# Second feed-forward stage on h times its weight, with the norm's scale at the gate

## The reference

```python
h = h + 0.5 * rmsnorm(swiglu(rmsnorm(h, gn[0]), ffn_w_in[0], ffn_w_out[0]), gn[1])   # first stage, 272 tokens
h = h + rmsnorm(mlstm_mixer(rmsnorm(h, gn[2]), ...), gn[3])                          # mixer
h = h + 0.5 * rmsnorm(swiglu(rmsnorm(h, gn[4]), ffn_w_in[1], ffn_w_out[1]), gn[5])   # second stage, 256 tokens
for l in range(2):                                                                   # two conditioned layers
    shift, scale, gate = split(silu(c) @ w_ada[l] + b_ada[l], 3)
    y = rms_norm(h, pre_norm_g[l]) * (1.0 + scale) + shift
    mix = attention_and_convolution(y @ w_in[l]) @ w_out[l]
    h = h + gate * rms_norm(mix, post_norm_g[l])

def rmsnorm(x, g):    # per token: x * rsqrt(mean(x * x) + 1e-6) * g
def swiglu(x, w_in, w_out):
    gu = x @ w_in
    return (silu(gu[..., :2816]) * gu[..., 2816:]) @ w_out
```

## Time and profile before

| | us |
|---|---|
| median of 3 runs | 833.57 (833.28 to 833.63) |
| profiled execution, whole time | 833.62 |
| its span (first to last instruction) | 831.7 |
| PE matmul busy / PE weight load busy | 803.1 / 777.6 |
| DVE busy | 584.6 |
| ACT busy | 418.5 |
| POOL busy | 128.0 |
| mean granted TensorE clock | 0.995 |
| DMA read and written | 158.96 MB |

### The profile page before, as it was taken

One profiled execution on the slowest core, in us unless ns is written; L12 is line 12 of the kernel. 1 busy time (PEld: TensorE's weight loads), 2 busy tenths in 40 slices (PEclk: granted clock), 3 DMA queues, 4 the chain that ended last, 5 costly groups with the idle time before them and its releaser, 6 DMA issues.

```text
span 831.7 us, 15721 instructions
## 1 busy us (share of the span) xinstructions
PE 803.1 (97%) x6436; PEld 777.6 (93%) x6436; DVE 584.6 (70%) x946; ACT 418.5 (50%) x716; POOL 128.0 (15%) x138
## 2 busy tenths in 40 slices
PE   7999999999999999999999999999999999999996
PEld 7999999999899899999999999989888999898895
DVE  6777776798687875788777768775666468566543
ACT  7544444445257665555444454445654365464541
POOL 3000000032210000010000012220235202025413
PEclk9999999999999999999999999999999999999998
DMA  9876676776245632459888775517444451734421
GB/s 326 295 254 221 226 249 242 226 274 201 88 143 185 196 112 93 152 186 340 291 287 270 275 238 185 184 51 256 150 124 150 154 173 55 259 130 147 131 76 51
DMA packets 45751, 158.96 MB, mean 191 GB/s; under 512 B 5064, under 2 KB 7624, under 8 KB 45680
## 3 DMA queue, kind: packets, MB, share of 16 engines
q1 hardware_dynamic: 45680, 157.96, 56.7%
HBM read 156.88 MB, written 1.06 MB: 190 GB/s over the span
## 4 chain that ended last, share of the span: by engine, by line
PE 76%; DVE 14%; ACT 6%; issue 2%; DMA 1%; POOL 1%; SPq 0%; DVEq 0%; ACTq 0%; POOLq 0%
PE ps L112 69%; PE ps L114 7%; DVE w L114 3%; ACT w L114 2%; DVE u L114 2%; DVE tmp L114 2%; DVE yg L114 1%; DVE Sb L114 1%; DVE st L114 1%; DVE cv L114 1%; ACT SW L114 1%; ACT Sb L114 1%; ACT L114 1%; DMA raw<-wst 1%; POOL rst L114 1%
## 5 line engine op out<-in xcount | busy, mean ns | idle before, releaser
L112 PE MATMUL ps<-u,w 128*128 128x256 f32 (+1 forms) x3887 | 499.9, 285 | 3.1 <-DVE w L114 1.6
L112 PEld LDWEIGHTS ps<-u,w 128*128 128x128 f32 x3887 | 481.9, 188 | 11.3 <-DVE w L114 4.0
L114 DVE TENSOR_TENSOR w<-raw,w 128x1024 fp32r<-128x1024 f32 x245 | 297.4, 1225 | 168.0 <-ACT w L114 161.6
L114 ACT CAST w<-raw 128x1024 fp32r<-128x1024 f32 x245 | 254.8, 1050 | 135.5 <-PE ps L114 124.8
L112 PE MATMUL ps<-h,w 128*128 128x272 f32 (+1 forms) x1000 | 130.4, 285 | 0.0
L112 PEld LDWEIGHTS ps<-h,w 128*128 128x128 f32 x1000 | 126.1, 188 | 0.1
L114 POOL TENSOR_TENSOR sqa<-sqa,sq 128x256 f32<-128x256 f32 (+1 forms) x22 | 23.1, 1050 | 358.3 <-ACT sq L114 357.8
L114 POOL TENSOR_SCALAR Sb<-Sb,st 128x256 f32<-128x256 f32 x32 | 42.9, 1355 | 111.1 <-DVE st L114 111.1
L114 DVE SCALAR_TENSOR_TENSOR acc<-adr,cact,acc 128x1024 f32<-128x1024 f32 x42 | 56.4, 1353 | 0.3 <-DMA adr<-wada 0.3
L114 PE MATMUL ps<-u,w 128*128 128x256 f32 (+1 forms) x169 | 48.1, 284 | 0.0
L112 PE MATMUL ps<-m,w 128*128 128x256 f32 x368 | 46.7, 281 | 0.0
(11 more groups left out here) (175 smaller groups left out, 692.2 us busy)
## 6 DMA issues: line engine op xcount, KB each, us to landing
raw<-wst SPq DMA_DIRECT2D x245, 512.0 KB, 4.6
adr<-wada SPq DMA_DIRECT2D x48, 512.0 KB, 4.0
Bt<-bias_rows SPq DMA_DIRECT2D x8, 192.0 KB
hT<-xT SPq DMA_DIRECT2D x4, 272.0 KB, 4.9
outT<-hT SPq DMA_DIRECT2D x2, 384.0 KB, 2.6
outT<-hT SPq DMA_DIRECT2D x1, 256.0 KB, 2.6
cs<-cst SPq DMA_DIRECT2D x1, 140.0 KB, 6.3
cs<-cst SPq DMA_DIRECT2D x1, 128.0 KB, 7.2
```

The costliest lines, as they stand in the source:

```text
L112: fn()
L114: fn().then_inc(m[0], m[1])
```

## The change

The second stage now works as the first does. u1 and u2 are made of the new h times the weight, without the second scale. The second scale is still made, and used in two places: as the factor r0 at each gate, and, since the up half and so the stage's output stay unscaled, through eps in the next norm: eps0 = (mean square + eps) * eps, which the first conditioned layer's boundary adds in place of eps.

- rms_pair is cut in two. rms_first makes the first scale; rms_second the mean square and the second power, without its transposes.
- add_and_weigh takes the place of add_and_normalise at this boundary. For each k: yg times the scale and the addition as before; then ACT writes u1 = h * gain, and DVE writes u2 = h * gain - u1. rms_second and the eps0 product stand behind the second addition in the queues.
- Its spread_scale goes to head as a hook: ahead of the head's fifth k PE transposes the second scale into bank 5, and DVE copies it into r0.
- In ffn both stages multiply the gate by r0 on DVE (zg), and silu reads zg.
- The second stage's modulation steps follow the first's pattern: 14 in the gates' loop (before 21), and 3, 3, 2 and 2 behind the first four output rows (before 1, 1, 1 and 0).

```diff
@@ rms_pair
-        def rms_pair(n, eps_of=None):
+        def rms_first(n, eps_of):
...
             dense(4)
-            r1 = spread(6, n, rst, m1)
+            state["bc"] = r1 = spread(6, n, rst, m1)
+            return r1, m1, mc
+
+        def rms_second(n, m1, mc):
...
             m2 = state["pow2"] = pool(partial(nc.gpsimd.tensor_tensor, rst2[:, 0:nt], msh[:, 0:nt], eps3[:, 0:nt],
                                               ALU.pow), mt, state.get("bc2"))
+            return m2, mt
+
+        def rms_pair(n, eps_of=None):
+
+            r1, m1, mc = rms_first(n, eps_of)
+            m2, _ = rms_second(n, m1, mc)
             dense(6)
-            r2 = spread(5, n, rst2, m2)
-            state["bc"], state["bc2"] = r1, r2
+            r2 = state["bc2"] = spread(5, n, rst2, m2)
             return r1, r2
@@ new, behind add_and_normalise
+        def add_and_weigh(n, off, ygm, hm, gain):
+
+            r1, m1, mc = rms_first(n, None)
+            mul, res, scale = {}, {}, {}
+
+            def scaled(k):
+                mul[k] = dve(partial(nc.vector.tensor_tensor, yg[:, k, 0:n], yg[:, k, 0:n], ps[:, 6, 0:n], ALU.mult),
+                             r1, ygm[k])
+                eng, e = (dve, nc.vector) if k in (0, 4) else (pool, nc.gpsimd)
+                res[k] = eng(partial(e.tensor_tensor, hT[:, k, off:off + n], hT[:, k, off:off + n], yg[:, k, 0:n],
+                                     ALU.add), mul[k], hm[k])
+
+            scaled(0)
+            for k in range(KT):
+                if k < KT - 1:
+                    scaled(k + 1)
+                if k == 0:
+                    scale["pow"], m = rms_second(n, m1, mc)
+                    dve(partial(nc.vector.tensor_scalar, eps0[:, 0:2], msh[:, 0:2], EPS, None, ALU.mult), m)
+                h, u = hT[:, k, off:off + n], u1[:, k, 0:n]
+                um1[k] = act(partial(nc.scalar.mul, u, h, gain(k)), res[k], ustate["use"])
+                um[k] = dve(partial(nc.vector.scalar_tensor_tensor, u2[:, k, 0:n], h, gain(k), u.bitcast(F32),
+                                    ALU.mult, ALU.subtract), um1[k])
+            free[6] = mul[KT - 1]
+
+            def spread_scale(i):
+                if i == KT // 2:
+                    m = state["bc2"] = spread(5, n, rst2, scale["pow"])
+                    first["r"] = free[5] = dve(partial(nc.vector.tensor_copy, r0[:, 0:n], ps[:, 5, 0:n]), m)
+
+            return [res[k] for k in range(KT)], spread_scale
@@ ffn
-                head(x1, x2, n, um1, um, nb=4)
+                head(x1, x2, n, um1, um, hook=hook, nb=4)
...
-                if j and (n == S or j % 3):
+                if j % 3:
                     ada_step(acc)
...
-                if n == S:
-                    s = free[bg] = act(partial(nc.scalar.activation, si[:, i, :], ps[:, bg, 0:n], ACT.Silu), mg,
-                                       hfr[i])
...
-                    z = free[bg] = dve(partial(nc.vector.tensor_tensor, zg[:, i, :], ps[:, bg, 0:n], r0, ALU.mult),
-                                       mg, first["r"], sir[i])
-                    s = sir[i] = act(partial(nc.scalar.activation, si[:, i, :], zg[:, i, :], ACT.Silu), z, hfr[i])
+                z = free[bg] = dve(partial(nc.vector.tensor_tensor, zg[:, i, 0:n], ps[:, bg, 0:n], r0[:, 0:n],
+                                           ALU.mult), mg, first["r"], sir[i])
+                s = sir[i] = act(partial(nc.scalar.activation, si[:, i, :], zg[:, i, 0:n], ACT.Silu), z, hfr[i])
...
-                while j < 4 and 0 < ad["use"] % 24 < ((17, 20, 22, 24) if n == T else (22, 23, 24, 24))[j]:
+                while j < 4 and 0 < ad["use"] % 24 < (17, 20, 22, 24)[j]:
@@ calls
-        hm = add_and_normalise(S, 16, ygm, hm, vg(4), None)
+        hm, hook = add_and_weigh(S, 16, ygm, hm, vg(4))
...
-        ygm = ffn(S, lambda j: gh[:, 8 + j:9 + j], guard, hm, 16, w_ffn[1])
+        ygm = ffn(S, lambda j: gh[:, 8 + j:9 + j], guard, hm, 16, w_ffn[1], hook)
...
-                                   lambda k: mod[:, 24 * l + k:24 * l + k + 1], m_G[l])
+                                   lambda k: mod[:, 24 * l + k:24 * l + k + 1], m_G[l], None if l else eps0)
```

More of the change, by code:

```diff
@@ L515, in rms_pair @@
                         state["sum"], state.get("pow"))
-                m = dve(partial(nc.vector.tensor_tensor, sst[0:16, 2:3], ps[0:16, 7, 4:5], eps_of[0:16, 2:3],
-                                ALU.add))
+                if nt == 3:
+                    m = dve(partial(nc.vector.tensor_tensor, sst[0:16, 2:3], ps[0:16, 7, 4:5], eps_of[0:16, 2:3],
+                                    ALU.add))
             m1 = state["pow"] = pool(partial(nc.gpsimd.tensor_tensor, rst[:, 0:nt], sst[:, 0:nt], eps3[:, 0:nt],
@@ L528, in rms_pair @@
             dense(4)
-            r1 = spread(6, n, rst, m1)
+            state["bc"] = r1 = spread(6, n, rst, m1)
+            return r1, m1, mc
+        def rms_second(n, m1, mc):
+            nt = len(sum_tiles(n))
             rows = [P, P, 16]
@@ L745, in build, with ffn @@
         br_m = {}
-        def ffn(n, gh_of, guard, hm, off, gw):
+        def ffn(n, gh_of, guard, hm, off, gw, hook=None):
             fx = ExitStack()
```

## The result

The changed kernel takes 835.32 us (median of 11, 834.09 to 837.12), the kernel before 833.36 (11, 832.94 to 834.19): ratio 1.0024, 95% interval 1.0015 to 1.0032. It is slower by 1.96 us, just above the 0.2% that count as a change. It is inside the stated range (832.8 to 835.8), 1.2 us above the forecast 834.1, above the forecast's own 834.9, and of the three outcomes it is the one that had 18%.

The account below looks back on a forecast made before the run. PE, busy 97% of the span, bounds the kernel, so what counts is when chunk 6 can start. The head's 1.37 us gain is lost on DVE's queue: 833.57 + 0.54 = 834.1, stated range 832.8 to 835.8.

Parts of the forecast that it names:

- stated range: Whole kernel's time: 832.8 to 835.8 us, leaving out the clock case and a tail below.
- the forecast's own 834.9: Upper end of the range 833.3 to 834.9 for the forecast as it stands, which was given 64%.
- the three outcomes: Against a 0.2% threshold (1.67 us): faster than 831.9, 3%; slower than 835.2, 18%; within, 79%.
- The new start of the head: Second stage's first matmul on PE starts at 352.78, 1.37 us earlier than before.
- The low part is late next: At the head, first u2 ends at 354.4; PE runs 8 matmuls, waits 0.7 us, resumes at 354.42.
- The Trainium skill's rule on POOL's power: At the boundary, the second power would block the first u2, 0.46 later: 834.6; rival with 5%.
- The tail and the gates: Behind the head, DVE's queue delays chunk 6's split to 368.70 and its PE start to 369.97: net +0.54 us.
- Main loop and moved steps: Gates' loop and first four output rows: extra products and seven moved steps cost nothing; steps up to 2 us without cover.
- The clock: Rival: the clock falls in PE's 1.9 us stall before chunk 6, costing 2.3 us: 836.4; 15%.
- The argument against it: Against a clock fall: at the kernel's end, where it fell, the idle time had no dense work on either side.
- granted clock 1.00 throughout: Sign expected in the profile: the clock stays at full over the whole kernel.
- 1.9 around it: Time outside the profiled span of 831.7 us, 1.9 us in the kernel before.

Follow-up runs that it names:

- experiment 5: Changed kernel with 16 dummy matmuls behind PE's last transposes, where nobody waits for them: 834.08 us, ratio 1.0014.
- experiment 4: Changed kernel with weight chunks 6 and 7 split earlier, ahead of the second gate's product: 833.43 us, span 830.3.
- experiment 3: Changed kernel with the second stage's modulation steps put back where they were before: 835.99 us.
- experiment 9: Changed kernel with six more dummy matmuls in PE's gap ahead of the head and 16 at PE's end: 834.26 us.
- experiment 7: Kernel before without 23 dummy calls: five at the end, and six between the two scales' transposes at each 256-column boundary: 835.27 us.
- experiment 2: Changed kernel with 16 dummy matmuls filling PE's stall between block 5 and chunk 6: 834.48 us, ratio 1.0012.

## Why the prediction was right, and where it fell short

- **The new start of the head** was right: 352.83 on the clock of before against 352.78.
- **The low part is late next** was right: the first u2 ends at 354.36 (354.4) and PE resumes at 354.42 (354.42), though POOL's addition did not slip in between the two pairs: it began beside the first and held the second up until 353.27.
- **The Trainium skill's rule on POOL's power.** In this trace as in the earlier trace rows the power does not block a DVE operation with two SBUF inputs: u2 keeps its 0.48. The Trainium skill (SBUF — State Buffer, "Who interferes with whom") would have it wait; the measurement decides. For the addition the rule holds (msh 0.71 for 0.35).
- **The tail and the gates.** Split of chunk 5 at 363.16 (363.04), product at 364.83 (364.63), hf at 365.74 (365.5), split of chunk 6 at 368.98 (368.70), chunk 6 at 370.25 (369.97). Each step is right, the sum 0.28 short: 0.1 in the tail, the rest 0.05 here and there between dependent steps. The net is +0.82, not +0.54, and the same in three profiles (21.77, 21.78 and, in experiment 5, 21.75 us from the mixer's last matmul to chunk 6, against 20.95 before); experiment 4 shows that the order of DVE's queue is the cause. One wait was not forecast: block 5 waits 0.17 us for the first gate's product on DVE, which frees its bank (before, silu on ACT did). It costs nothing, since PE waits for chunk 6 behind it. The head's end is right (365.24 against 365.2).
- **Main loop and moved steps** at nothing: right, by the trace and by experiment 3.
- **The clock.** This was the rival with 15% and 2.3 us. The mechanism is real: behind a stall of 1.8 us the clock fell in one profile (experiment 9) and stayed at full in four (the changed kernel's two, experiments 3 and 5), and the spell cost 1.5 us. What failed is the step that gave the kernel as a whole a chance of it; it is a thing of single executions. The argument against it was misread too: the idle time at the kernel's end does have dense work on one side, PE being busy for 8.00 of the 8 us ahead of 822. The sign "granted clock 1.00 throughout" could not come, since the kernel before itself has 0.53 and 0.62 from 686 to 690 (the changed one 0.69 and 0.50).
- **How much of the median is the clock's** is not shown. Of the 43 executions with the bare stall of 1.8 us 16 have a mean clock of 0.993 or less, and most of them are longer; but so have 2 of 11 with the stall filled and 3 of 11 with the stall gone, where the one that was profiled has its low clock at 220 to 228. In the gap ahead of the head the clock is low in 4 of the 10 profiles of the changed stage, and in none of the three of the kernel before that keep their six dummies between the two scales' transposes (experiment 7 took them out); whether taking these dummies away costs something in the changed kernel was not tested. And in experiments 5 and 9, with the stall as bare as ever, the median span is 0.9 above that of before, which the queue's 0.8 explains alone.
- **The sum's last term**, "1.9 around it", failed: it was carried over from before. It is 2.6 in the changed kernel, 0.7 us of the 1.96, and experiment 5 gives it back without touching the work.
- **The range.** The bounds added up in the sum were 833.3 to 834.9, and the measured 835.32 lies above them. The stated range held because it was drawn 0.9 wider at the top, for which the prediction gives no term; that is luck.

Taken together: 0.8 us from the queue (0.5 in the profiled span, since that execution came 0.3 early), 0.7 outside the span, and a rest of about 0.4. Spells of low clock in a part of the executions are a likely part of that rest, in the stall (1.5 us each) and in the gap ahead of the head (0.5 in experiment 3); it is only what is left over, and how it divides stays open.

## What to carry to other kernels

When a wait is taken off the head of a stage, follow each engine's queue to the first moment after it at which the bottleneck engine runs out of prepared input: the gain is real only if that moment comes earlier too, and two lines that reorder the queue can be worth more than the edit. An idle gap on TensorE cost its length in every execution here and a spell of low clock in some, so compare medians of many executions and their spread, not one profile. And look at what lies outside the span before you look for the cause of a loss of 0.1 or 0.2% in the work.

## What the runs showed of the hardware that was not expected

- 16 dummy matmuls behind the end of all of PE's work take 0.7 us off the time outside the span (2.58 to 1.90). In the fourteen profiled executions 1.9 us lie outside where no piece of code comes behind 829 (ten of them), 2.3 where one queue's does (one), and 2.9 to 3.4 where both queues' do (three).
- The granted clock also falls at the boundaries between stages in single executions. In experiment 2 it is 0.50 from 351 to 353, in experiment 3 0.54 from 350 to 352; PE has little but dummies to do there, but chunk 6 starts 0.4 and 0.5 us later. In experiment 4 the spell from 220 to 228 cost 0.3: from the first stage's last matmul to the mixer's last are 132.67 us, against 132.30 to 132.42 in the twelve profiles with the clock at full there.
- A stall of 1.8 us was enough for the clock to fall in one of five profiled executions; in the profile of before the attention's waits of up to 1.2 us left it at full.
